# Down weights of the last but one expert as eleven transfers of 8 and 48 partitions

## The chip, the cores and the metric

The kernel runs on one core of a Trainium2 chip. The time is that of the device, in microseconds, the median of several runs. The engines are TensorE (PE in the rows, PEld for its weight loads), VectorE (DVE), ScalarE (ACT), GpSimd (POOL) and SyncE (SP), which here does little but wait and issue DMA transfers. The core has 16 DMA engines.

## The reference, cut to what matters

The program is one layer of a decoder with 256 prompt rows and 8 sample rows: a mixing part (projection, pooling, attention), then a mixture of 32 experts, then a norm. What matters here is the mixture:

```python
def expert_step(acc, p):
    w1, w3, w2, ge = p
    hdn = jax.nn.silu(xf @ w1) * (xf @ w3)
    return acc + ge[:, None] * (hdn @ w2).astype(jnp.float32), None

acc, _ = lax.scan(expert_step, jnp.zeros((N, D), jnp.float32), (w_gate, w_up, w_down, gate.T))
```

`w_gate` and `w_up` are 1024 x 512 for each expert, `w_down` is 512 x 1024, all float32, 2 MB a matrix. A token goes to two experts, so an expert has few of the 264 tokens, but all its weights are needed: 32 x 3 x 2 MB.

## The kernel before

The mixing part fills about the first 290 us. Then the kernel goes through the experts 0 to 31 in order. For each one TensorE multiplies a block of 32 gathered tokens: gate and up (`gate_up`, L1363, 64 matmuls), a transpose of the result (`turn_hidden`, L1371), the gathering of the tokens of the next expert (L1347, L1355), down (`down`, L1379, 32 matmuls), and `combine` (L1388 and L1394), which adds the expert's rows to the sums in PSUM. VectorE and ScalarE make the hidden rows between them (L1225, L842, L1230) and copy the product of down out (L1235).

The weights stand in ten slots of SBUF, 16 KB in each of 128 partitions (`ring` has nine of them, `x9` is the tenth, named x in the trace). SP issues one transfer for each matrix, in the order of `ORDER`, when the matrix that stood in the slot ten places earlier has been used (`slot_used`). Each slot has one semaphore, `s_slot[q]`; a transfer adds 16 to it, and `arrived[item]` is the count at which an item has landed. The order is gate, up, down for the experts 0 to 29, and at the end

```python
[(LAST - 1, 0), (LAST - 1, 1), (LAST, 0), (LAST, 1), (LAST - 1, 2), (LAST, 2)]
```

with `LAST` = 31. Gate and up of expert 31 come as four half transfers (L561, semaphores `s_last[0]` to `[3]`), its down weights as four quarters (L565, `s_last[4]` to `[7]`). All transfers of weights are on SP's one queue.

TensorE's order at the end is: gate and up of 30, combine of 29, turn of 30, tokens of 31, gate and up of 31, turn of 31, down of 30 (`down_rows(LAST - 1)`), combine of 30, down of 31 in four quarters with a wait for each, combine of 31. So down of 30 stands behind gate and up of 31, as its weights do in the queue. `down_rows` waits for the hidden rows and for the weights:

```python
pe.wait_ge(s_hE, e + 1)
pe.wait_ge(s_slot[home[e, 2]], arrived[e, 2])
```

After the last combine come squares, a root (`L871`, `L1297`, `L910` to `L914`), the scaling and the stores of y_prompt (L576, L578) and y_sample (L581).

Down weights are laid out with partition p holding two groups g of two rows c of 1024 elements (`"(g p c) n -> p g (c n)"`), so a partition receives two pieces of 8 KB.

Of the kernel before, what the change touches and what calls it, by code (L numbers as in the profile page):

```python
# [12 lines left out]
P = 128  # L13
# [4 lines left out]
NS = 8  # L18
# [33 lines left out]
NSLOT = RING + 1  # L52
FRONT = 6
LAST = EXPERTS - 1
ORDER = [(e, m) for e in range(LAST - 1) for m in range(3)] + [(LAST - 1, 0), (LAST - 1, 1), (LAST, 0), (LAST, 1), (LAST - 1, 2), (LAST, 2)]
# [59 lines left out]
def build(nc, t):  # L115
# [4 lines left out]
    with ctx:  # L120
# [3 lines left out]
        def sem(name):  # L124
            return ctx.enter_context(nc.semaphore(name))
# [4 lines left out]
        slot = [ring[:, n * SLOT:(n + 1) * SLOT] for n in range(RING)] + [x9[:]]  # L130
# [196 lines left out]
        for item in STREAM:  # L327
            q = last_step.index(min(last_step))
# [7 lines left out]
        SLOT_BASE = list(slot_count)  # L336
# [3 lines left out]


        home = {item: FREED[n % NSLOT] for n, item in enumerate(ORDER)}
        arrived = {item: SLOT_BASE[home[item]] + 16 * (n // NSLOT + 1) for n, item in enumerate(ORDER)}
        later_home = [home[0, m] for m in range(3)]
        later_base = [SLOT_BASE[q] + 16 * sum(home[item] == q for item in ORDER if item[0] < LAST) for q in later_home]
        dead = slot[home[LAST - 3, 2]]
        yst = dead[:, 0:2 * D].rearrange("p (b n) -> p b n", b=2)
        sqend = dead[:, 3 * D:]
# [13 lines left out]
        for step, a in PLAN:  # L362
# [10 lines left out]
            elif step == "forget":  # L373
                assign(PART, "forget")
            elif step == "bias":
                assign(SCORES, "bias")
            elif step == "pool":
                assign(QB, "pool")
            elif step in ("dmax", "dshift", "datt"):
                assign(CHAIN, step, a)  # L380
            elif step == "dpv":
                assign(PART, "dpv", a)
            elif step == "dsums":
                assign(SUM, "den")
            elif step in ("mix", "gate", "up", "merge"):
                assign(None, step, a)
            elif step in ("scores", "pT"):
                for f in range(2):
                    assign((PAIR if step == "scores" else PAIRT)[f], step, a, f)
            elif step == "pv":  # L390
                assign(TR, "pv", a)
            elif step == "out":
                for half in range(2):
                    assign((PART, QB)[half], "opart", half), assign(SUM, "osum", half)
                for i in range(4):
                    assign((BIG0, BIG1, SCORES, TR)[i], "out", i)
            elif step == "norm":
                for i, (b, _, _) in enumerate(TPOSE):
                    assign(b, "hT", i)
            elif step == "route":  # L400
                assign(PART, "logits"), assign(SUM, "logits0"), assign(BIG0, "ranks"), assign(PART, "tables")


        s_slot = [sem(f"slot{i}_loaded") for i in range(NSLOT)]
# [79 lines left out]
        def load_matrix(eng, e, m, q):  # L484

            src = t[("w_gate", "w_up", "w_down")[m]][0, bass.ds(e, 1)]
            if m < 2:
                eng.dma_start(slot[q], src.rearrange("e (p k) f -> p (e k f)", p=P)).then_inc(s_slot[q], 16)
            else:
                eng.dma_start(slot[q].rearrange("p (g n) -> p g n", g=2), src.rearrange("e (g p c) n -> p (e g) (c n)", g=2, p=P)).then_inc(s_slot[q], 16)  # L490
# [15 lines left out]
        def _(sp):  # L506
# [3 lines left out]
            for kind, a in LOADS:  # L510
# [4 lines left out]
                item = kind, a  # L515
# [10 lines left out]
                else:  # L526
                    src = (t["w_up_pool"][0] if a == 0 else t["w_up_att"][0]) if kind == "up" else t["w_out"][0, a * DC:(a + 1) * DC]
# [16 lines left out]
            def slot_used(n):  # L544

                e, m = ORDER[n - NSLOT]
                sp.wait_ge(s_gu if m < 2 else s_dn, e + 1)

            for n in range(NSLOT, len(ORDER)):
                e, m = ORDER[n]  # L550
                q = home[e, m]
                slot_used(n)
                if e < LAST:
                    load_matrix(sp, e, m, q)
                elif m == 0:
                    slot_used(n + 1)
                    for half in range(2):
                        for gu_half in range(2):
                            src = t[("w_gate", "w_up")[gu_half]][0, LAST].rearrange("(p k) f -> p k f", p=P)
                            ks = slice(4 * half, 4 * half + 4)  # L560
                            sp.dma_start(slot[home[LAST, gu_half]].rearrange("p (k n) -> p k n", k=DK)[:, ks], src[:, ks]).then_inc(s_last[2 * half + gu_half], 16)  # L561
                elif m == 2:
                    src = t["w_down"][0, LAST].rearrange("(g p c) n -> p g c n", g=2, p=P)
                    for j in range(FC):
                        sp.dma_start(slot[q].rearrange("p (j n) -> p j n", j=FC)[:, j], src[:, j // 2, j % 2]).then_inc(s_last[4 + j], 16)  # L565
# [1194 lines left out]
```

## Time and profile before

| | |
|---|---|
| median of 3 runs | 725.45 us (725.09 to 727.71) |
| the profiled execution's own time | 723.92 us |
| its span, first to last instruction | 721.9 us |
| mean granted TensorE clock | 0.919 |
| TensorE busy | 599.4 us, 83% |
| VectorE busy | 223.3 us, 31% |
| DMA moved | 269.15 MB, 373 GB/s over the span |

The span is counted in us from the first instruction. Busy TensorE time is modelled and is not TensorE at its peak. The digits by slice are the busy share in tenths; 9 is 90% or more. All stretches below are of this one execution.

### The profile page before, as it was taken

Reading aid. Unit: us, or ns where it says so; the run is one execution under the profiler, and the core shown is the slowest. Engines: PE = TensorE matmul, PEld = TensorE weight load, DVE = VectorE, ACT = ScalarE, POOL = GpSimd, SP = SyncE. Lnnn points to the kernel's source line nnn. Section 1 sums busy time; section 2 is a strip of 40 time slices with the busy share of each in tenths; the row PEclk is TensorE's granted clock in tenths of the full one; section 3 lists DMA queues with packets and bytes.
Section 4 is the critical chain, followed back from the end, with each engine's and each line's share of the span. In section 5 each row is a group of like instructions: output and inputs, shape, how many; then the busy total and the mean of one; then the engine's idle time right before and its main releaser. Section 6 shows DMA issues by size and latency. Waiting matters only on the chain.

```text
span 721.9 us, 13750 instructions
## 1 busy us (share of the span) xinstructions
PE 599.4 (83%) x6157; PEld 367.1 (51%) x6157; DVE 223.3 (31%) x549; ACT 88.3 (12%) x232; POOL 51.1 (7%) x57
## 2 busy tenths in 40 slices
PE   4899999999999999999687768787677776787673
PEld 3688777776574455554344434343344433444341
DVE  4249779982131252322111111111111111111113
ACT  2211142221101230000000000000000000000003
POOL 4107412012000000000000000000000000000000
PEclk9999999999999999999888987799888988789898
DMA  9965989997999489999999999999999999999982
GB/s 300 303 260 203 347 146 402 359 377 300 414 422 414 199 313 366 425 426 419 424 427 427 422 422 429 427 423 421 426 427 424 423 424 424 428 425 424 422 368 88
DMA packets 41378, 269.15 MB, mean 373 GB/s; under 512 B 9844, under 2 KB 10672, under 8 KB 22879
## 3 DMA queue, kind: packets, MB, share of 16 engines
q1 hardware_dynamic: 28960, 229.34, 78.8%
q0 software_dynamic: 3072, 35.19, 11.9%
q10 hardware_dynamic: 9287, 3.73, 1.9%
q8 instruction: 50, 0.82, 0.5%
q14 instruction: 9, 0.07, 0.0%
HBM read 266.01 MB, written 2.46 MB: 372 GB/s over the span
## 4 chain that ended last, share of the span: by engine, by line
PE 50%; DMA 46%; DVE 1%; ACT 1%; issue 1%; ACTq 0%; DVEq 0%
DMA ring<-w_up 33%; PE bank L1363 10%; PE bank L1446 8%; PE bank L1538 8%; DMA x<-w_up 5%; DMA ring<-w_down 5%; PE bank L1584 4%; PE bank L1601 4%; DMA wf<-w_in 3%; PE bank L1379 2%; PE bank L1515 2%; PE bank L1347 2%; PE bank L1394 1%; PE bank L1522 1%; PE bank L1388 1%
## 5 line engine op out<-in xcount | busy, mean ns | idle before, releaser
L1363 PE MATMUL bank<-ring,front 128*32 128x256 f32 x1856 | 162.7, 486 | 85.8 <-DMA ring<-w_up 73.8
L1363 PEld LDWEIGHTS bank<-ring,front 128*32 128x32 f32 x1856 | 86.6, 138 | 144.9 <-issue 120.6
L1225 DVE COPY front<-bank 128x256 f32<-128x256 f32 x32 | 13.6, 424 | 233.2 <-PE bank L1363 233.2
L1446 PE MATMUL bank<-hT,ring 128*128 128x264 f32 x256 | 60.1, 393 | 0.0
L1538 PE MATMUL bank<-hT,ring 128*128 128x264 f32 x256 | 59.7, 389 | 0.4 <-ACT front L774 0.4
L1379 PE MATMUL bank<-ring,front 128*32 128x256 f32 x928 | 55.4, 379 | 0.2 <-DMA ring<-w_down 0.2
L842 ACT ACTIVATE front<-bank 128x128 f32<-128x128 f32 x32 | 8.9, 277 | 371.0 <-PE bank L1371 371.0
L1446 PEld LDWEIGHTS bank<-hT,ring 128*128 128x128 f32 x256 | 48.7, 193 | 9.6 <-issue 1.4
L1538 PEld LDWEIGHTS bank<-hT,ring 128*128 128x128 f32 x256 | 47.8, 190 | 9.7 <-issue 2.1
L1347 PE MATMUL bank<-front 128*32 128x256 f32 (+1 forms) x768 | 52.3, 385 | 0.2 <-DVE front L1129 0.2
L1019 DVE TENSOR_TENSOR ring<-ring,front 128x1024 f32<-128x1024 f32 x32 | 41.9, 1310 | 8.1 <-DMA front<-q_scratch 7.7
L1235 DVE COPY front<-bank 128x256 f32<-128x256 f32 x32 | 13.6, 424 | 87.0 <-PE bank L1379 87.0
L1379 PEld LDWEIGHTS bank<-ring,front 128*32 128x32 f32 x928 | 30.2, 110 | 20.2 <-issue 0.8
L1021 DVE TENSOR_REDUCE front<-ring 128x16 f32<-128x1024 f32 x32 | 39.0, 1220 | 1.1
L1363 PE MATMUL bank<-x,front 128*32 128x256 f32 x192 | 31.6, 502 | 8.7 <-DMA ring<-w_up 8.1
L1394 PE MATMUL bank<-front 32*128 32x256 f32 x512 | 36.7, 400 | 0.0
L1347 PEld LDWEIGHTS bank<-front 128*32 128x32 f32 (+1 forms) x768 | 18.3, 107 | 24.5 <-issue 18.4
L1394 PEld LDWEIGHTS bank<-front 32*128 32x128 f32 x512 | 23.1, 184 | 13.9 <-issue 13.2
L1601 PE MATMUL bank<-ring,hT 128*128 128x512 f32 x64 | 28.7, 599 | 0.0
L1363 PEld LDWEIGHTS bank<-x,front 128*32 128x32 f32 x192 | 14.7, 143 | 15.9 <-issue 13.6
L1230 DVE TENSOR_TENSOR front<-front,bank 128x128 f32<-128x128 f32 x32 | 9.2, 288 | 41.7 <-ACT front L842 41.7
L1388 PE MATMUL bank<-front 128*32 128x256 f32 x256 | 20.0, 380 | 1.1 <-DVE front L1235 1.1
(311 smaller groups left out, 525.3 us busy)
## 6 DMA issues: line engine op xcount, KB each, us to landing
ring<-w_gate SPq DMA_DIRECT2D x28, 2048.0 KB, 41.8
ring<-w_up SPq DMA_DIRECT2D x28, 2048.0 KB, 38.7
ring<-w_down SPq DMA_DIRECT2D x28, 2048.0 KB, 41.8
ring<-w_in SPq DMA_DIRECT2D x8, 2048.0 KB, 24.2
x<-w_gate SPq DMA_DIRECT2D x3, 2048.0 KB, 42.4
x<-w_up SPq DMA_DIRECT2D x3, 2048.0 KB, 37.8
x<-w_down SPq DMA_DIRECT2D x3, 2048.0 KB, 41.4
ring<-w_out SPq DMA_DIRECT2D x2, 2048.0 KB, 16.5
```

Of the source, the lines that this page charges most:

```text
L1019: v.tensor_tensor(ks, ks, qb[:, b % 2].unsqueeze(1).to_broadcast([P, 2, DC]), ALU.mult).then_inc(s_kprod, 1)
L1021: v.tensor_reduce(scs[:, b, 2 * pair:2 * pair + 2], ks.rearrange("p j (h d) -> p j h d", h=HEADS), AX.X, ALU.add).then_inc(s_kused, 1)
L1347: last = m.matmul(bank[GATHER][CAP * g:CAP * (g + 1), 0:QUART], sel[0:n, i, b], h2[0:n, b, g * QUART:(g + 1) * QUART], start=b == 2, stop= ...
L1363: last = m.matmul(bank[GATEUP][32 * g:32 * g + 32, 0:256], xgT[:, k % 2, k // 2], w[:, k, 256 * (g % 2):256 * (g % 2) + 256], start=k == 0 ...
L1379: last = m.matmul(bank[TDOWN][32 * g:32 * g + 32, 0:256], hE[:, j % 2, j // 2], wd[:, j, 256 * g:256 * g + 256], start=j == 0, stop=j == F ...
L1388: last = m.matmul(bank[SACC][CAP * g:CAP * (g + 1), 0:QUART], back[:, i, SEQ + CAP * g:SEQ + CAP * (g + 1)], ysb[:, i], start=False, stop= ...
L1394: last = m.matmul(acc[:, g, b], back[rows, i, b * P:(b + 1) * P], ysb[rows, i], start=False, stop=False, skip_group_check=True)
L1446: last = m.matmul(out[:, 0:TOK], w, hT[:, k, 0:TOK], start=k == 0, stop=k == DK - 1)
L1515: last = m.matmul(out[g:g + HEADS, :], scs[:, a, j], pages[:, j], start=j < 4, stop=j >= 4)
L1538: last = m.matmul(out[:, 0:TOK], w[:, k, cols], hT[:, k, 0:TOK], start=k == 0, stop=k == DK - 1)
L1584: last = m.matmul(out[:, 0:TOK], w[:, k, a * P:(a + 1) * P], src[:, k], start=k == 0, stop=k == CC - 1)
L1601: last = m.matmul(out[:], hT[:, k, b * P:(b + 1) * P], w[k // CC][:, k % CC, half * 512:(half + 1) * 512], start=k == 0, stop=k == DK - 1)
```

## The change

The item `(LAST - 1, 2)`, down weights of expert 30, is issued as eleven transfers by partition range: ten of 8 partitions (`NS` is 8) and one of the remaining 48. They go to the same place from the same addresses, on the same queue, at the same point of the order, and all add to the slot's semaphore; the counts waited for are made from the number of transfers. No other item is changed.

```diff
         home = {item: FREED[n % NSLOT] for n, item in enumerate(ORDER)}
-        arrived = {item: SLOT_BASE[home[item]] + 16 * (n // NSLOT + 1) for n, item in enumerate(ORDER)}
+        UNEVEN = (LAST - 1, 2)
+        SHORT = [slice(NS * n, NS * n + NS) for n in range(10)] + [slice(NS * 10, P)]
+        transfers = {item: len(SHORT) if item == UNEVEN else 1 for item in ORDER}
+        arrived = {item: SLOT_BASE[home[item]] + 16 * sum(transfers[i] for i in ORDER[n % NSLOT:n + 1:NSLOT]) for n, item in enumerate(ORDER)}
         later_home = [home[0, m] for m in range(3)]
-        later_base = [SLOT_BASE[q] + 16 * sum(home[item] == q for item in ORDER if item[0] < LAST) for q in later_home]
+        later_base = [SLOT_BASE[q] + 16 * sum(transfers[item] for item in ORDER if item[0] < LAST and home[item] == q) for q in later_home]
...
                 slot_used(n)
-                if e < LAST:
+                if (e, m) == UNEVEN:
+                    src = t["w_down"][0, e].rearrange("(g p c) n -> p g (c n)", g=2, p=P)
+                    for rows in SHORT:
+                        sp.dma_start(slot[q].rearrange("p (g n) -> p g n", g=2)[rows], src[rows]).then_inc(s_slot[q], 16)
+                elif e < LAST:
                     load_matrix(sp, e, m, q)
```

## Rows read from the trace of the kernel before

**Rows 1.** The page: SP's DMA queue, the chain that ended last, L1363's group.
```profile
q1 hardware_dynamic: 28960, 229.34, 78.8%
...
PE 50%; DMA 46%; DVE 1%; ACT 1%; issue 1%; ACTq 0%; DVEq 0%
...
L1363 PE MATMUL bank<-ring,front 128*32 128x256 f32 x1856 | 162.7, 486 | 85.8 <-DMA ring<-w_up 73.8
```

**Rows 2.** Stages: busy us by engine, then granted clock, DMA share, GB/s.
```profile
300.00:640.00 340.00, 262.92 (x3604) 143.18 (x3602) 51.53 (x176) 15.95 (x49) 0.00 (x0) 0.86 1.01 424
...
694.00:698.00 4.00, 3.05 (x44) 1.24 (x36) 0.76 (x4) 0.65 (x2) 0.00 (x0) 1.00 1.02 418
698.00:702.00 4.00, 3.66 (x64) 1.98 (x64) 0.22 (x2) 0.00 (x0) 0.00 (x0) 1.00 0.73 298
702.00:704.00 2.00, 1.44 (x22) 0.99 (x26) 0.95 (x3) 0.42 (x2) 0.00 (x0) 1.00 0.50 193
704.00:706.00 2.00, 1.46 (x28) 0.49 (x19) 0.42 (x1) 1.34 (x2) 0.00 (x0) 1.00 0.43 174
706.00:708.00 2.00, 2.00 (x36) 1.27 (x36) 0.00 (x0) 0.00 (x0) 0.00 (x0) 1.00 0.18 61
```

**Rows 3.** TensorE in order of time, gate and up of experts 29 and 30.
```profile
673.21 5.67 PE L1363 MATMUL bank<-ring,front 128*32 128x256 f32 x64 [5.40 <-DMA ring<-w_up]
...
688.13 5.04 PE L1363 MATMUL bank<-ring,front 128*32 128x256 f32 x64 [3.71 <-DMA ring<-w_up]
```

**Rows 4.** DMA busy tenths, 694 to 708 us in 40 slices of 0.35 us.
```profile
DMA  9999999999999989754655464454454432222300
```

**Rows 5.** TensorE in order of time, from gate and up of 31.
```profile
698.12 3.66 PE L1363 MATMUL bank<-ring,front 128*32 128x256 f32 x64 [0.58 <-DVE front L1138]
702.33 0.44 PE L1371 MATMUL bank<-cea,front 128*128 128x128 f32 x2 [0.55 <-DVE front L1225]
703.00 1.93 PE L1379 MATMUL bank<-ring,front 128*32 128x256 f32 x32 [0.23 <-DMA ring<-w_down]
...
707.12 1.94 PE L1379 MATMUL bank<-ring,front 128*32 128x256 f32 x32
```

**Rows 6.** SP in order of time: start, duration of the issue.
```profile
658.84 7.48 SPq L561 DMA_DIRECT2D ring<-w_up  x1
666.42 2.97 SPq L490 DMA_DIRECT2D ring<-w_down  x1
669.43 18.57 SPq L565 DMA_DIRECT2D ring<-w_down  x4
...
717.61 1.75 SPq L581 DMA_DIRECT2D y_sample<-front  x2
```

**Rows 7.** From issue to landing, L561 and then L565.
```profile
DMA to landing us min/median/max: 37.6/38.8/39.1
...
L565 SPq DMA_DIRECT2D ring<-w_down x4: 2112/3872/8591, 669.4 to 685.9; - x4
...
DMA to landing us min/median/max: 22.0/25.7/34.7
```

**Rows 8.** The chain that ended last, around the edited load.
```profile
666.42 36.45 DMA ring<-w_down
```

**Rows 9.** DMA packets from 717.5 to 722 us, the stores of the outputs.
```profile
DMA packets 352, 1.08 MB, mean 240 GB/s; under 512 B 64, under 2 KB 96, under 8 KB 352
...
q10 hardware_dynamic: 32, 0.02, 1.4%
```

**Rows 10.** DMA queues from 286 to 694 us: packets, MB, share.
```profile
q8 instruction: 35, 0.57, 0.6%
```

**Rows 11.** SP in order of time, x_sample, and loads from 254 to 317 us.
```profile
1.66 0.39 SPq L509 DMA_DIRECT2D x<-x_sample  x1
...
254.69 0.33 SPq L488 DMA_DIRECT2D ring<-w_up  x1
...
317.50 0.43 SPq L490 DMA_DIRECT2D ring<-w_down  x1
```

## The prediction

> **What bounds the kernel now.** I read the page first. TensorE is busy 83% of the span (the table above), but the chain that ended last is half DMA, most of it loads of expert weights through w_up and w_down, and TensorE's largest idle time is in front of the gate and up matmuls, L1363, released by a w_up load [rows 1]. The reader is to see a weight stream that paces the experts. The table of stages says the same: from 300 to 640 us the DMA share is full and 424 GB/s arrive, and 418 still up to 698 us [rows 2]. With three matrices of 2 MB an expert, TensorE waits in each late expert: 5.40 and 3.71 us in front of gate and up of 29 and 30, released by w_up [rows 3].
>
> But the edit touches only the last transfers but four, so what counts is the end. There the order of the stream is gate and up of expert 30, gate and up of expert 31 in four parts (L561), down of expert 30 (L490, the one edited), and down of expert 31 in four parts (L565). Next I read the table at 694 to 708 us. The rate falls from 418 GB/s to 298, then 193 and 174, then 61 [rows 2], and the shares by slice stay near 5 tenths before they fall [rows 4]: half of the sixteen DMA engines have finished and the other half have not. So the engines are not level. Taking 425 / 16 = 26.6 GB/s an engine, the 298 GB/s over 698 to 702 is full rate for 1.6 us and half rate for the rest (425 x 1.6 + 212 x 2.4 = 1189 against 298 x 4 = 1192), so the early half ends at 699.6 us on average. After 702 us 193 x 2 + 174 x 2 + 61 x 2 = 856 KB are left; at 212 GB/s that is 4.0 us, so the late half ends at 706.0 us. The lag is 6.4 us. A load counts as landed when the slowest engine is through, so the kernel waits for the late half every time.
>
> Then the engine's own order at the end. Gate and up of expert 30 at 688.13 wait for DMA [rows 3]. Gate and up of expert 31 at 698.12 wait for VectorE (0.58 us), not for DMA, whose last part, issued at 658.84, landed by 658.84 + 39.1 = 697.94 at the latest [rows 5 to 7]: a near tie. The down matmuls of expert 30 start at 703.00, with 0.23 us of wait on the edited load [rows 5], which landed at 666.42 + 36.45 = 702.87 [rows 8]. The down matmuls of expert 31 start at 707.12 with no wait [rows 5]. After them comes a chain of combine, squares, root and output that no load touches.
>
> **The change, part by part.** (1) The data. A row of one partition is 16 KB, at 26.6 GB/s 0.616 us. As one transfer of 128, each engine moves 8 rows. An eight-partition transfer takes eight engines with one row each: in the output stretch there are two y_prompt transfers of 128 rows and four y_sample transfers of eight, and the packets under 512 B (one per engine that completes) are 64 = 2 x 16 + 4 x 8; the 32 packets of queue q10 are two transfers of 8 rows and 8 completions [rows 9]. So ten short transfers put ten rows on one set of eight engines, and the one of 48 gives three to each of sixteen: 13 rows on the one half, 3 on the other. Each half moves by 5 rows, 5 x 0.616 = 3.1 us. That is just half the lag of 6.4. If the short transfers fall on the early half, the early half ends at 702.7 and the late one at 702.9: level.
>
> Which half they fall on no grouped row tells. Something has put unequal work on the engines, and the queue that carries single packets, not sixteen alike, is the instruction queue: 35 packets, 0.57 MB, between 286 and 694 us [rows 10], while q1 moves whole matrices. If they go to eight engines only, they are 0.57 MB / 8 = 71 KB each, 2.7 us at 26.6 GB/s an engine, the order of the lag (an estimate). In the packet records around 36 to 50 us, where a next packet starts on an engine as the one before it ends, I followed the engine that took an instruction packet, and it seems not to be one of the eight that took the eight-row write of the queries. That following goes wrong when two packets end together, so I give it weight but not certainty. It says: short transfers on the early half.
>
> The Trainium skill (DMA: Bandwidth & Descriptors, section Why a DMA increments its semaphore by 16 and not by 1) says that a hardware-queued transfer uses the largest number of engines up to 16 that divides its outer dimension, and the lowest-numbered ones: eight for 8 rows, sixteen for 48. The trace agrees as to the eight; by that rule the same 5 rows move and the sum is the same, while by a split over all sixteen it would be 725.4.
>
> (2) What becomes of the 3.1 us. Only loads behind the short transfers move: down of 30 and the four parts of down of 31. Down of 30 lands at 702.87 - 3.1 = 699.8 instead. But TensorE is busy until 702.33 + 0.44 = 702.77 with L1371, which waits for VectorE (0.55 us) and that for gate and up of 31 [rows 5]. So the down matmuls can start 703.00 - 702.77 = 0.23 us sooner and no more. Expert 31's down then starts at 706.9, its last quarter at 706.9 + 3/4 x 1.94 = 708.35; its load landed at 685.9 + 22.0 = 707.9 before [rows 7], so it was already in time. Gate and up of 31 are in front of the edit in the queue and don't move. From this profile: -0.23 us.
>
> The upper bound of the gain: the profiled execution took 723.92 us (span 721.9 and 2.0 around it), the median is 725.45, so 1.53 more. If all of that is a weight stream which is later against TensorE, down of 30 waits 0.23 + 1.53 = 1.76 us, and since gate and up of 31 begin with their first half (698.12 + 1.83 = 699.95, while the last part would land at 699.47) nothing else waits; all 1.76 us would be given back. If it is anything else, 0.23. I take 0.55, nearer to the low end, which is what a row shows.
>
> (3) Ten more issues on SP. Unhindered, an eight-row issue took 0.39 us (x_sample), two y_sample ones 1.75 together, 0.88 each [rows 6, 11]. Eleven are 4.3 to 9.7 us, against the 2.97 us of the one transfer now: 1.3 to 6.7 us more. Behind them on SP stand only the four L565 issues. Those now sit in SP for 18.57 us for 2 MB, and the last is issued 22.0 us before it lands [rows 6, 7]: SP is ahead of the stream, and its stall is room in the queue, not work. 6.7 us out of 22 are covered by that lead. Without the cover the parts of 31 would be late by what is left over. (4) Completions: 80 more tiny packets (11 transfers with 10 x 8 + 16 completions against 16), from q1's rows 8 on an engine, nothing to weigh against 0.616 us rows. Waits keep their place, the count waited for is only larger. Nothing on TensorE, VectorE, ScalarE or GpSimd is added.
>
> Sum: -0.23 to -1.76, taken -0.55: 725.45 - 0.55 = 724.9 us.
>
> **Rivals.** *A, the short transfers fall on the late half.* Then the late half gets 3.1 us more: down of 30 lands at 705.95, its matmuls start at 706.1, 3.1 us late; down of 31 at 710.2, its last quarter at 711.65, after its load's 707.87 + 3.1 = 710.95, so nothing on top. 725.45 + 3.1 = 728.5. What I followed in the packet records is all that speaks against it. It decides at the first of the ten: any row more on the late half is late by 0.62 us. *B, the transfers are spread over all sixteen.* Then nothing changes, 725.4; against it stand the 64 completions. *C, the issue is dear.* If each of eleven issues stalled like the four L565 ones, 18.57 / 4 = 4.64 us, they would take 51 us in place of 2.97, and the parts of down 31, issued until 688.0 now, would be issued until 736; landing some 2 us later, they would set the end at about 725.45 + 738 - 708.6 = 755 us. It becomes slower from the point where the eleven take more than 2.97 + about 20 us. Against it: the stalls fit room for packets (an engine gets 9 packets from a part, 3 from a short transfer and the eight other engines none), and from 254 to 317 us load issues took 0.33 to 0.43 us [rows 11].
>
> The Trainium skill (DMA: Bandwidth & Descriptors, sections Anatomy of one DMA and Rules for kernel authors) speaks against the change: join small transfers, since each has a fixed cost near 2.0 us. An estimate from that page, were the ten extra paid one behind the other: 20 us, 745 us. The trace has parts of 512 KB whose landings follow one another much closer than their own 22.0 to 34.7 us in the queue [rows 7], so fixed costs overlap here.
>
> **How the numbers follow.** Short transfers on the early half, gain 0.2 to 1.8 us: 0.77. A: 0.12. B: 0.08. C in any size: 0.03. The likeliest one's time is 724.9, its own range 723.5 to 725.5. The range for all takes in A, the only other sizeable case with a price, and the spread of a run: 723.2 to 728.8 (the three runs before reach from 725.09 to 727.71). About 0.5%, 3.6 us, is what this measurement can tell from no change. Only a gain above the bound of 1.76 would be faster by that: 0.03. Slower by that is C, and a third of A (3.1 us with a bad run): 0.07. The rest, 0.90, is same.
>
> **What would show it.** Right: q1 has 80 more packets, 28960 + 80 = 29040 [rows 1]; in 698 to 702 us the rate stays near 420 GB/s and the DMA is through at about 705 us, not 708; the stretch at half rate is gone; L1379 of expert 30 has no wait on w_down and starts 0.2 us sooner after L1371; gate and up of 31 stand where they were. A shows the half-rate stretch twice as long, to 711 us, and a wait of 3.3 us before L1379. B shows the same half-rate stretch and q1's count more than 80 up. C shows long issues at the new line and a hole in the DMA share before 708. The prediction would be wrong if the lag of the halves isn't there without a profile, if TensorE's near tie at 698.12 is decided otherwise, or if one engine of the early half was late enough that 13 rows make it last.

## The result, and the profile after

Over all runs of both kernels the median is 739.87 us after (738.87 to 741.28, 4 runs) and 725.27 us before (722.45 to 727.71, 4 runs): a ratio of 1.0204, with a 95% interval of 1.0182 to 1.0226. The change costs 14.6 us, where 0.5 us less was forecast. The profiled execution took 740.48 us, with a span of 738.1 us against 721.9 before. One of the twelve executions of the kernel with every second partition (experiment 2), 762.71 us at a granted clock of 0.80, was in a slower state of the chip, and its ratio is made without it.

The page of the kernel after, its queue and its chain:

```profile
q1 hardware_dynamic: 29040, 229.34, 78.6%
...
DMA 47%; PE 46%; DVE 3%; SPq 1%; issue 1%; ACT 1%; ACTq 0%; DVEq 0%
```

The count of packets is the predicted one, 80 more than in [rows 1]: each short transfer used eight engines. Now the stages of the kernel after (columns as in [rows 2]):

```profile
640.00:686.00 46.00, 33.23 (x444) 17.63 (x444) 6.11 (x20) 1.95 (x6) 0.00 (x0) 0.85 1.01 424
686.00:690.00 4.00, 1.05 (x12) 0.68 (x16) 0.00 (x0) 0.00 (x0) 0.00 (x0) 0.66 1.01 420
690.00:694.00 4.00, 4.00 (x43) 2.03 (x36) 0.00 (x0) 0.00 (x0) 0.00 (x0) 0.50 1.05 235
694.00:698.00 4.00, 4.00 (x66) 2.12 (x62) 1.10 (x3) 0.28 (x1) 0.00 (x0) 0.99 1.02 244
698.00:702.00 4.00, 2.93 (x46) 1.23 (x38) 0.49 (x2) 0.37 (x1) 0.00 (x0) 1.00 1.05 212
702.00:706.00 4.00, 0.02 (x3) 0.00 (x0) 0.00 (x0) 0.00 (x0) 0.00 (x0) 0.79 0.89 157
706.00:710.00 4.00, 3.24 (x32) 1.57 (x32) 0.00 (x0) 0.00 (x0) 0.00 (x0) 0.50 0.86 159
```

The rows from 690 us on are the ones to look at. The rate there is a little over half of what it was, 235 and 244 GB/s, while the DMA share stays at 1.05 and 1.02. Before, a low rate came with a low share (193 GB/s at 0.50, [rows 2]): half of the engines had finished. Here all are busy and each is slow. The packet records of the two traces say the same: from 690 to 694 us a packet of 8 KB takes 0.31 us before (median of 200), and 0.58 us after (median of 112, the shortest 0.41), so that not one engine still ran at its old rate. The two columns have to be read together; the rate alone looks alike.

TensorE of the kernel after, in order of time:

```profile
688.95 6.19 PE L1370 MATMUL bank<-ring,front 128*32 128x256 f32 x64 [4.18 <-DMA ring<-w_up]
...
700.09 1.93 PE L1370 MATMUL bank<-ring,front 128*32 128x256 f32 x32 [0.58 <-DVE front L1145]
706.76 3.64 PE L1370 MATMUL bank<-ring,front 128*32 128x256 f32 x32 [4.74 <-DMA ring<-w_up]
...
717.46 3.64 PE L1386 MATMUL bank<-ring,front 128*32 128x256 f32 x32 [5.99 <-DMA ring<-w_down]
...
723.28 1.93 PE L1386 MATMUL bank<-ring,front 128*32 128x256 f32 x32
```

The second half of gate and up of expert 31, which is ahead of the edited load in the queue, waits 4.74 us for w_up, and down of expert 30 waits 5.99 us for w_down, where [rows 5] had 0.23. The 32 matmuls of that down take 3.64 us in place of 1.93. The stages around it show why:

```profile
712.00:716.00 4.00, 0.00 (x0) 0.00 (x0) 0.16 (x1) 1.49 (x2) 0.00 (x0) 0.82 0.67 211
716.00:720.00 4.00, 2.54 (x25) 1.39 (x29) 0.00 (x0) 0.00 (x0) 0.00 (x0) 0.50 0.13 51
```

TensorE stood still from 711.47 to 717.46 us, and the granted clock was 0.50 from 716 to 720, the lower of its two levels. The same had happened once before: it stood still for most of 702 to 706, the clock was 0.50 from 706 to 710, and the 32 matmuls at 706.76 took 3.64 us as well. The chain that ended last, and SP in order of time:

```profile
680.90 36.42 DMA ring<-w_down
717.32 0.14 issue
```
```profile
666.77 15.90 SPq L559 DMA_DIRECT2D ring<-w_down  x11
682.71 11.73 SPq L572 DMA_DIRECT2D ring<-w_down  x4
```

The edited load has landed at 717.32 instead of 702.87 [rows 8]: 14.45 us. The slow matmuls behind it add 3.64 - 1.93 = 1.71. Together that is 16.16 of the 16.2 us between the two spans. So the question is why that load is 14.45 us late.

### The profile page after: what moved, and what is told of

The parts are those of the page before. It is cut to its first block, busy times and chain, and to the rows that moved or that the text cites. A ratio compares the mean times of both kernels' runs of the same rounds, so it can differ in the third digit from the quotient of the medians.

```text
span 738.1 us, 13760 instructions
## 1 busy us (share of the span) xinstructions
PE 604.2 (82%) x6157; PEld 368.7 (50%) x6157; DVE 223.2 (30%) x549; ACT 88.5 (12%) x232; POOL 50.6 (7%) x57
## 4 chain that ended last, share of the span: by engine, by line
DMA 47%; PE 46%; DVE 3%; SPq 1%; issue 1%; ACT 1%; ACTq 0%; DVEq 0%
DMA ring<-w_up 32%; PE bank L1370 9%; PE bank L1453 8%; DMA x<-w_up 5%; PE bank L1545 5%; DMA ring<-w_down 5%; PE bank L1591 4%; PE bank L1608 4%; PE bank L1386 3%; DMA wf<-w_in 2%; DMA front<-q_scratch 2%; PE bank L1522 2%; PE bank L1354 2%; SPq L559 1%; PE bank L1401 1%
## 5 line engine op out<-in xcount | busy, mean ns | idle before, releaser
L1370 PE MATMUL bank<-ring,front 128*32 128x256 f32 x1856 | 165.2, 496 | 93.7 <-DMA ring<-w_up 82.4
L1232 DVE COPY front<-bank 128x256 f32<-128x256 f32 x32 | 13.6, 424 | 241.2 <-PE bank L1370 241.2
L1386 PE MATMUL bank<-ring,front 128*32 128x256 f32 x928 | 57.1, 388 | 6.0 <-DMA ring<-w_down 6.0
L1242 DVE COPY front<-bank 128x256 f32<-128x256 f32 x32 | 13.6, 424 | 94.5 <-PE bank L1386 94.5
L1370 PE MATMUL bank<-x,front 128*32 128x256 f32 x192 | 28.5, 463 | 6.3 <-DMA ring<-w_up 5.7
L1370 PEld LDWEIGHTS bank<-x,front 128*32 128x32 f32 x192 | 14.1, 131 | 11.4 <-issue 8.4
```

The source lines that it names most:

```text
L1370: last = m.matmul(bank[GATEUP][32 * g:32 * g + 32, 0:256], xgT[:, k % 2, k // 2], w[:, k, 256 * (g % 2):256 * (g % 2) + 256], start=k == 0 ...
L1386: last = m.matmul(bank[TDOWN][32 * g:32 * g + 32, 0:256], hE[:, j % 2, j // 2], wd[:, j, 256 * g:256 * g + 256], start=j == 0, stop=j == F ...
```

## The experiments

Every edit is to the load of down of expert 30, unless another expert is named. "Before" is the median of the kernel before on the same chip.

**1. Destination or source, short transfers or the rest.** Eight short transfers (partitions 0 to 63) and one of the upper 64, with neighbouring rows or rows 4 apart on either side.

```
SHORT = [slice(8 * n, 8 * n + 8) for n in range(8)] + [slice(64, P)]                               # neighbours
SHORT = [slice(32 * (n // 4) + n % 4, 32 * (n // 4) + 32, 4) for n in range(8)] + [slice(64, P)]   # 4 apart
sp.dma_start(dst[rows], src[from_rows])   # dst and src each with one of the two lists
```

Neighbours on both sides:

> Eight short transfers to 8 neighbouring partitions and one of 64. The theory of the destination (eight engines that write to 8 neighbouring partitions share two places of entry into SBUF, so that a short transfer of 128 KB moves at 2 x 26.6 GB/s and takes 2.4 us in place of 0.62): 8 x 2.4 in place of 10 x 2.4, so four fifths of the changed kernel's loss, +10 to +13 us, and the same long packets of 8 KB, 0.57 us and more against 0.31. The theory of the source (reading close together in HBM): the same. A fixed cost for each transfer: 9 against 11, +12 us. The lag of the engines taken the wrong way round: at most +2.5 us.

4 apart on both sides:

> The same number of transfers with the same sizes, but the 8 partitions of a short one are 4 apart, at both ends; the result is the reference's. Destination: each of the eight engines writes to an entry of its own, packets of 8 KB take 0.31 us as in the kernel before, the loss is gone: -0.2 to -1.8 us against before, and the stretch at half rate at the end is shorter by 2 x 2.5 us. Source: gone too, if 4 apart is far enough for it, otherwise still +10. Fixed cost for each transfer: still +12 us. Lag the wrong way round: +2.5 us.

To neighbours, from rows 4 apart:

> Destination 8 neighbouring partitions, source rows 4 apart; the down weights of expert 30 end up in partitions that aren't theirs, so that one expert's rows come out otherwise; work and bytes are the same. Destination: as c0, +10 to +13 us. Source: as before, within 2 us. Fixed cost: +12 us.

To partitions 4 apart, from neighbours:

> Destination partitions 4 apart, source rows neighbouring; again the down weights of expert 30 in partitions that aren't theirs. Destination: no loss, -0.2 to -1.8 us against before. Source: as c0, +10 to +13 us. Fixed cost: +12 us.

Measured, in this order, with before at 725.14: 740.61 (ratio 1.0213, 1.0181 to 1.0245), 737.47 (1.0168, 1.0121 to 1.0215), 740.17 (1.0218, 1.0181 to 1.0255) and 735.63 (1.0151, 1.0117 to 1.0185). The stages of the second, 4 apart on both sides:

```profile
690.00:694.00 4.00, 4.00 (x68) 2.16 (x60) 0.40 (x2) 0.00 (x0) 0.00 (x0) 0.85 1.03 391
694.00:698.00 4.00, 3.42 (x44) 1.59 (x44) 0.75 (x4) 0.65 (x2) 0.00 (x0) 1.00 1.03 240
698.00:702.00 4.00, 1.93 (x32) 0.94 (x32) 0.44 (x2) 0.00 (x0) 0.00 (x0) 1.00 1.00 171
```

With destinations 4 apart, 391 GB/s (387 in the fourth kernel) still arrive from 690 to 694 us; with neighbours it was 229 in the first and 230 in the third. In the source no such difference shows. So the destination decides. But where the theory of the destination had no loss at all, 12.3 and 10.5 us stayed, of 15.5 and 15.0: behind the short transfers the rate falls to 240 and 171 all the same. The suspect left was the rest, one transfer to the upper 64 partitions, which has no short transfer in it.

**2. Which splits are free.** An entry is here a place through which engines write into SBUF. The theory tested from here on is that the 128 partitions are reached through sixteen of them, each for four neighbouring partitions and the four that are 32 further on, and that an entry takes in little more than one engine brings. No row moves between engines in any of these four, since each transfer has sixteen rows or a multiple.

```
SHORT = [slice(0, 64), slice(64, P)]                        # d1
SHORT = [slice(0, P, 2), slice(1, P, 2)]                    # d2
sp.dma_start(slot[q][:, 512 columns], ...)  # eight times, 128 partitions each: d3
SHORT = [slice(16 * n, 16 * n + 16) for n in range(8)]      # d4
```

The two halves, 0 to 63 and 64 to 127:

> Two transfers, partitions 0 to 63 and 64 to 127, sixteen engines each: no engine gets more rows than another, and there is only one issue more. Theory of entries (the 128 partitions are reached through sixteen entries at about 27 GB/s each, neighbouring groups of four on different ones, the lower 64 and the upper 64 on eight each): each half goes through eight entries and takes twice its time, so down of 30 takes about 9.8 us of the queue in place of 4.9, and more where the early and the late engines meet on the same entries: +3 to +8 us. Rows moved between engines as the cause: no loss. Cost for each transfer (about 14.6 / 10 = 1.5 us): +1.5 us at most.

Every second partition:

> Two transfers, the even and the odd partitions: again two, 64 rows each on sixteen engines, but each spans all the entries, eight rows an entry in all. Entries: two engines share two entries by turns, so little or nothing is lost, within 2 us of before and well under d1. If d1 loses through the halving itself (two transfers, 4 rows an engine), d2 loses the same.

Eight transfers of 128 partitions:

> Eight transfers of all 128 partitions with 2 KB of each: eight issues, eight completions an engine, each engine on its own entry. Entries: nothing lost, within 1.5 us. Cost for each transfer: 7 x 1.5 = +10 us.

Eight of sixteen neighbours:

> Eight transfers of 16 neighbouring partitions, sixteen engines with one row each: no rows moved between engines. Entries: 256 KB through four entries at 106 GB/s, 2.4 us each, 19.3 us for the eight in place of 4.9: +12 to +16 us. Rows moved between engines as the cause: no loss. Cost for each transfer: as d3, +10 us.

Measured, with before at 725.62: 739.17 (ratio 1.0165, 1.0129 to 1.0201), 725.77 (0.9994, 0.9970 to 1.0017), 725.34 (0.9994, 0.9971 to 1.0017), 739.71 (1.0191, 1.0149 to 1.0233). Stages of the halves, then of every second partition:

```profile
690.00:694.00 4.00, 4.00 (x40) 2.23 (x44) 0.00 (x0) 0.00 (x0) 0.00 (x0) 0.50 1.09 250
694.00:698.00 4.00, 4.00 (x65) 2.11 (x54) 0.85 (x3) 0.28 (x1) 0.00 (x0) 0.96 0.99 225
698.00:702.00 4.00, 2.92 (x46) 1.43 (x46) 0.74 (x3) 0.37 (x1) 0.00 (x0) 1.00 0.98 225
```
```profile
690.00:694.00 4.00, 4.00 (x44) 2.13 (x40) 0.00 (x0) 0.00 (x0) 0.00 (x0) 0.50 1.00 414
694.00:698.00 4.00, 4.00 (x62) 2.08 (x54) 0.88 (x3) 0.28 (x1) 0.00 (x0) 0.93 1.01 414
```

Two transfers in halves cost as much as the change; two of every second partition, of the same bytes and packets, cost nothing, and eight of 128 partitions neither (their packets are of 2 KB, and the rate from 694 to 698 us was 355 GB/s, but nothing waited for it). That settles two things: a transfer more has no price in time here, and uneven engines are not needed for the loss. The halves lost 13.6 us where 3 to 8 were expected: they lose, as the theory of entries said, but its size was wrong. The eight of sixteen neighbours lost 14.1 us, inside the 12 to 16 expected.

**3. Which partitions share.** With entries as above, a step of 8 reaches eight of sixteen entries and a step of 4 reaches all, though both span the whole 128.

```
SHORT = [slice(n, P, 8) for n in range(8)]   # f1, sixteen rows each
SHORT = [slice(n, P, 4) for n in range(4)]   # f2, 32 rows each
```

> The load of down of expert 30 as eight transfers of sixteen partitions that are 8 apart (0, 8, 16 ...; 1, 9, 17 ...), so that each transfer reaches over the whole 128, and no row moves between engines against sixteen neighbouring ones (739.7). Theory of entries of four neighbouring partitions, where (partition divided by 4) modulo 8 and the half of 64 name the entry: each transfer touches eight of sixteen entries, as a half of 0 to 63 does, so the rate falls to about 220 GB/s and the time is 735 to 740; if the engines drift so that even and odd transfers mix, less, 728. Theory that only a narrow range of partitions is slow: full rate, 725.5, as for every second partition.

> Down of expert 30 as four transfers of 32 partitions that are 4 apart. Against the eight transfers of 16 that are 8 apart (737.8, ratio 1.0161) each transfer now reaches all sixteen groups that (partition divided by 4) modulo 8 and the half of 64 name, two rows in each. If those groups are the entries that engines share: full rate of about 415 GB/s up to 698 us and 725.5 to 726.5. If it is any transfer of less than 64 partitions, or the number of partitions that a transfer skips: 735 to 740.

Measured: 737.76 for the step of 8 (before 726.41, ratio 1.0161, 1.0128 to 1.0194), 724.21 for the step of 4 (before 724.99, 0.9991, 0.9971 to 1.0011). Stages of the one, then of the other:

```profile
690.00:694.00 4.00, 3.95 (x52) 2.32 (x56) 0.00 (x0) 0.00 (x0) 0.00 (x0) 0.66 1.07 281
694.00:698.00 4.00, 4.00 (x66) 2.12 (x62) 1.10 (x3) 0.28 (x1) 0.00 (x0) 1.00 0.99 201
```
```profile
690.00:694.00 4.00, 4.00 (x58) 2.58 (x48) 0.04 (x1) 0.00 (x0) 0.00 (x0) 0.69 1.01 416
694.00:698.00 4.00, 3.51 (x52) 1.66 (x44) 1.06 (x3) 0.65 (x2) 0.00 (x0) 1.00 1.01 414
```

Not how far a transfer reaches, but how many entries it touches, decides.

**4. The disputed cost by itself.** Behind the last weight load of the kernel before, loads with nothing beside them: first single ones, then streams of four. Each kernel was executed once, 754.83 and 790.90 us with the loads added.

```
for rows in (slice(0, P), slice(0, 64), slice(0, P, 2), slice(0, 16), slice(0, 8), slice(0, 32, 4), slice(0, 4)):   # p1
    sp.dma_start(idle[rows], wsrc[rows]).then_inc(s_probe, 16)
    ...   # waits for it
for rows in (slice(0, 8), slice(0, 32, 4), slice(0, 16), slice(0, P, 8), slice(0, 64), slice(0, P, 2)):             # p2
    for k in range(4):
        sp.dma_start(idle[k][rows], wsrc[k][rows]).then_inc(s_probe, 16)
    ...   # waits for the four
```

> The kernel before, and behind its last weight load seven loads of 16 KB rows one after the other, each alone (waited for before the next): 128 partitions, 0 to 63, the 64 even ones, 0 to 15, 0 to 7, eight that are 4 apart from 0, and 0 to 3; they lengthen the kernel and write a buffer that nothing reads any more. With about 2 us from issue to the first byte: if a row costs 0.62 us on its engine wherever it goes, the landings take 4.9 + 2, 2.5 + 2, 2.5 + 2, then 0.6 + 2 for each of the other four. If neighbouring partitions share an entry of about one engine's rate: 0 to 63 takes 4.9 + 2 and the even ones 2.5 + 2; 0 to 15 (four entries, four rows each) 2.5 + 2; 0 to 7 (two entries) 2.5 + 2 as well; eight that are 4 apart 0.6 + 2; 0 to 3 (one entry) 2.5 + 2.

> The kernel before, and behind its last weight load six groups of four loads of 16 KB rows to four buffers, each group alone: rows 0 to 7; eight rows 4 apart from 0; rows 0 to 15; sixteen rows 8 apart; rows 0 to 63; the 64 even ones. They lengthen the kernel. Engines with a row a transfer need 2.5 us for the first four groups and 9.8 us for the last two, plus about 3 us of start and landing. If groups of four partitions are entries of hardly more than one engine's rate (27 GB/s): 524 KB to two entries 9.7 us, to eight 2.5; 1 MB to four entries 9.7 us, to eight 4.9; 4 MB to eight entries 19.4 us, to sixteen 9.8. If a narrow destination only costs at the start of a transfer, as the single loads alone let one think (0 to 7 came 3.8 us after its issue, eight rows 4 apart 3.1): 2.5 to 4 us in all of the first four, and the last two alike.

The single loads left it half open. SP in order of time shows when each was issued, and the next one's issue follows its landing:

```profile
709.68 0.38 SPq L572 DMA_DIRECT2D ring<-w_down  x1
718.28 0.66 SPq L574 DMA_DIRECT2D ring<-w_down  x1
726.12 0.61 SPq L576 DMA_DIRECT2D ring<-w_down  x1
731.51 0.34 SPq L578 DMA_DIRECT2D ring<-w_down  x1
735.70 0.28 SPq L580 DMA_DIRECT2D ring<-w_down  x1
739.47 0.81 SPq L582 DMA_DIRECT2D ring<-w_down  x1
742.57 0.25 SPq L584 DMA_DIRECT2D ring<-w_down  x1
```

The 64 lower partitions took 726.12 - 718.28 = 7.84 us and the 64 even ones 5.39: 2.45 us more, the size of four rows (4 x 0.616). But eight neighbours took 3.77 and eight that are 4 apart 3.10, where the theory wanted 1.85 us between them. A single short load is mostly start and landing: in the packet records the eight neighbours' first packet starts 0.88 us after the issue, and the last ends 1.57 us before the next issue. In the streams that share is smaller; their six stretches are, in the order of the code:

```profile
713.10:721.70 8.60, 2.46 (x34) 1.18 (x26) 5.14 (x13) 4.67 (x12) 0.00 (x0) 0.89 0.50 63
724.90:728.30 3.40, 0.00 (x0) 0.00 (x0) 0.00 (x0) 0.00 (x0) 0.00 (x0) 0.50 0.42 142
729.60:738.50 8.90, 0.00 (x0) 0.00 (x0) 0.00 (x0) 0.00 (x0) 0.00 (x0) 0.50 0.97 116
741.30:746.50 5.20, 0.00 (x0) 0.00 (x0) 0.00 (x0) 0.00 (x0) 0.00 (x0) 0.50 0.87 194
748.70:769.40 20.70, 0.00 (x0) 0.00 (x0) 0.00 (x0) 0.00 (x0) 0.00 (x0) 0.50 0.98 203
771.70:782.60 10.90, 0.00 (x0) 0.00 (x0) 0.00 (x0) 0.00 (x0) 0.00 (x0) 0.50 0.94 381
```

Eight neighbours (two entries) 63 GB/s, eight that are 4 apart (eight entries) 142; sixteen neighbours (four entries) 116, sixteen 8 apart (eight) 194; 64 neighbours (eight) 203, 64 even ones (sixteen) 381. That is 24 to 32 GB/s an entry, save in the second, which is too short for its start and end to be small. It is about the rate of one engine, 26.6. The packet records of the same trace are plainer still. A packet of 8 KB took 0.31 us (median) for the 64 even rows and for the eight that are 4 apart, 0.64 for 0 to 63 and for the sixteen 8 apart, and 1.20 for the eight and for the sixteen neighbours. If the rows are dealt to the engines evenly and in order, that is one, two and four engines at an entry. The expected 9.7, 2.5, 9.7, 4.9, 19.4 and 9.8 us came out as 8.6, 3.4, 8.9, 5.2, 20.7 and 10.9. In experiments 2 to 4 the rows read change along with the partitions written; that the source plays no part rests on experiment 1.

The Trainium skill (SBUF — State Buffer, section Door 1: The DMA port swizzle) gives just this map: sixteen ports, named by (partition divided by 4) modulo 8 and by the half of 64, of 435 GB/s together. By that, eight neighbours have two ports and, an estimate, 54 GB/s; the trace has 63. The same page says further on (section "Can I just issue two DMAs to hit both halves?") that one transfer over all 128 partitions is the only way to reach all sixteen; here the traces disagree: steps of 2 and of 4 kept 414 to 416 GB/s in the stream, and the 64 even rows had 381 alone.

**5. Is it a matter of the end of the stream?** The halves of run d1, for down of expert 20.

```
-        UNEVEN = (LAST - 1, 2)
+        UNEVEN = (20, 2)
```

> The load of partitions 0 to 63 and then 64 to 127 again, but for the down weights of expert 20 (in the middle of the stream, where 424 GB/s arrive from 440 to 540 us) instead of expert 30. At expert 30 about 220 GB/s arrived for some 20 us, in which those 2 MB and the 2 MB behind them came, and the kernel took 13.6 us more. Theory that only the two halves themselves are slow: 2 MB at 225 in place of 424 GB/s, 9.3 in place of 4.9 us, 4.4 us later for all that follows: about 730. Theory that the engines stay out of step for as long as the next 128-partition loads follow one another: the low rate goes on well past 2 MB, and each 2 MB more costs 4.4 us; at four matrices 743, for the rest of the stream (some 30 matrices) over 800. Theory that it is a matter of the end of the stream alone: no loss, 725.5.

Measured: 736.53 against 726.41 (ratio 1.0165, 1.0128 to 1.0202), 10.1 us. Its stages:

```profile
520.00:530.00 10.00, 8.07 (x106) 4.95 (x110) 1.10 (x3) 0.28 (x1) 0.00 (x0) 0.83 1.01 426
530.00:540.00 10.00, 2.81 (x50) 1.39 (x41) 0.99 (x4) 0.37 (x1) 0.00 (x0) 0.82 1.03 241
540.00:550.00 10.00, 7.45 (x90) 4.14 (x90) 0.81 (x2) 0.00 (x0) 0.00 (x0) 0.67 1.02 224
550.00:560.00 10.00, 3.96 (x59) 1.90 (x58) 1.29 (x5) 0.65 (x2) 0.00 (x0) 0.85 0.98 407
```

For 20 us the rate is 241 and 224 GB/s, 4.65 MB that 424 would bring in 11.0 us: 9.0 us lost, and the stream never gets them back. None of the three theories gave the size: the halves are 2.1 MB, and the low rate lasts for a bit over twice that, then ends by itself.

**6. Can levelling pay at all?** Twelve rows to one set of eight engines and four to the other (meant: the early and the late), with all sixteen entries in use over the whole load.

```
SHORT = [slice(32 * (n // 2) + 2 * (n % 2) + 1, 32 * (n // 2) + 32, 4) for n in range(4)] + [slice(0, P, 2)]
SHORT += [slice(32 * (n // 2) + 2 * (n % 2) + 1, 32 * (n // 2) + 32, 4) for n in range(4, 8)]
```

For expert 30, and then for expert 29, in front of matmuls that wait for the stream:

> Down of expert 30: 64 rows that are two apart in one transfer, and ahead of and behind it eight transfers of eight rows that are 4 apart, so twelve rows on the early eight engines and four on the late eight: 4 x 0.616 = 2.5 us of the 6.4 us lag are moved each way. If the engines are the limit and the destination is all that cost time in the change made: the half-rate stretch between about 699 and 706 us shrinks, the last packet lands some 2.5 us earlier, and the time is 0.2 to 1.8 us lower, 724 to 725.3. If the sixteen entries on the memory's side are the limit (their full rate hardly above the engines'), the eight transfers take eight engines to eight entries and the rest waits: nothing gained or a few us lost, 725.5 to 730. If uneven work on the engines itself slows all: as the change made, 737.

> The split of the run e2_level4_at30 (731.9, ratio 1.0085), put into down of expert 29, ahead of gate and up of expert 30, which wait for the stream. If engines that are level gave time back, here all 2.5 us would show: 723. If, as after e2_level4_at30 seemed, any split in which engines write elsewhere than in a transfer of 128 makes them meet others at the same entry, the rate is about 250 GB/s for some 12 us and the kernel loses 5 to 8 us: 731 to 734. If the loss in e2 was only in the last transfers of the stream: 725.5.

Measured: 731.85 (before 726.41, ratio 1.0085, 1.0054 to 1.0115) and 732.64 (before 724.99, 1.0088, 1.0063 to 1.0112). Stages of the first:

```profile
690.00:694.00 4.00, 4.00 (x69) 2.50 (x58) 0.81 (x2) 0.00 (x0) 0.00 (x0) 1.00 1.00 413
694.00:698.00 4.00, 2.93 (x43) 1.32 (x46) 0.78 (x3) 0.65 (x2) 0.00 (x0) 1.00 1.07 252
698.00:702.00 4.00, 1.63 (x35) 0.84 (x28) 0.00 (x0) 0.00 (x0) 0.00 (x0) 1.00 0.89 247
```

Less lost than with neighbours, but lost, at both places. Moving the four rows gave nothing back even where the stream binds. The theories that said 723 to 725.5 fall. At expert 30 the time is also over the 725.5 to 730 that the theory of entries had there; at expert 29 it is inside the 731 to 734 that was expected once the first was known.

## Why the prediction was wrong

**The step that failed** is the first number of part (1): "A row of one partition is 16 KB, at 26.6 GB/s 0.616 us", taken to hold wherever the row goes. It was read from a stream in which every transfer goes to all 128 partitions, and there it holds. A short transfer to eight neighbours has two entries. In the stream of four it took 8.60 / 4 = 2.15 us each; ten are 21.5 us where the sum had ten rows, 6.2 us. That is 15.3 us more work for the eight engines that carry them than was counted (an estimate, since other loads run beside them), and the edited load came 14.45 us later than before, where it was to come 3.1 us sooner. The clock, which the sum had no term for, added 1.71 us. The transfer of 48 behind them reaches the eight entries of the upper half only, and so is slow in its turn, as the upper 64 were in experiment 1.

**Right:** eight engines a short transfer, from the completions in [rows 9]; q1's count shows it. **Right in what it concluded, not in its number:** part (3). The eleven issues took 15.90 us, more than the 9.7 that I had as the most, and the four behind them 11.73 in place of 18.57; SP was through at 694.4 us, 6.4 later than before, and the last parts came well after that. Rival C, the dear issue, is refused by the eight transfers of 128 partitions as well: their issues took 26.12 us, and the time was 725.34.

**Not put to the test:** part (2) with its gain of 0.23 to 1.76 us, and the five rows moved each way. The slow entries came over them before a level finish could show. On which half the short transfers fall no run measured. Rival A named the right sign, but with 3.1 us for rows that are only more on one side, and in experiment 2 the loss is there without any row moved. Rival B (no change) is out.

**Wrong:** "Gate and up of 31 are in front of the edit in the queue and don't move." Their second half came in for a wait of 4.74 us. The place in the queue protects only on an engine's own list. The early engines are ahead of the late ones by the 6.4 us of lag, and when they turned to the edited load the late ones still had gate and up of 31 to bring. That all engines then ran at about half rate, the late ones too, is in the packets (0.58 us in place of 0.31 from 690 to 694 us, none under 0.41); that they were held by entries which the early ones filled is the reading that fits, not one that a run isolated.

**What the Trainium skill said against the change** (DMA: Bandwidth & Descriptors, section Anatomy of one DMA) came to 20 us in the prediction's estimate, from a fixed cost of 2.0 us a transfer; the section has that figure for transfers issued from GpSimd, and these are issued from SP. The loss is near, the reason isn't: eight transfers of 128 partitions cost nothing.

**Open:** why the low rate in experiment 5 lasts for twice the bytes of the halves, and in d1 as well; engines 6.4 us apart, of which some are in the halves while others are in front of or behind them, would stretch it, but that is argued. And what made the level split lose 5 to 8 us: its last four short transfers write to the upper half. If early engines carry them and the late engines are still writing there, the two meet, and in the first four, to the lower half (413 GB/s from 690 to 694 us), they don't; no run showed which engines write where.

## What to carry to other kernels

In a full stream, split a load by columns or by a step of 2 or 4 partitions, not by ranges: here the same 2 MB in two halves cost 13.6 us, in every second partition nothing. Before a row's time is carried over to a transfer of another shape, look at what it writes to as well as at who carries it, and read the rate beside the share: full share at half rate is a jam, half share at half rate is an engine that has finished. Where entries are hardly faster than engines, be wary of levelling a lag by giving some engines' rows to others: those rows still have to go in through the same entries. The two levelled runs, 0.9% slower each, fit that, but do not prove it.

## What the runs showed of the hardware that I had not expected

A load with few entries slows loads that are not its own: 424 GB/s in all fell to 225 for about 20 us, for 2.1 MB of edited data (g1, d1). A wait that this brings in can be dearer than it looks: behind its wait of 5.99 us, down of expert 30 ran at a granted clock of 0.50 and took 3.64 us in place of 1.93. And a single short load hides it: alone, eight neighbours took 3.77 us and eight that are 4 apart 3.10; in a stream of four, 63 against 142 GB/s.
